# Attention with compressed values for two heads at once: a 256-column block diagonal, and its transposition in an earlier step and another bank

## The reference, cut to what matters

```python
kc = compress(k_cmp, pe_ck, w_ck1, w_ck2)      # 31 blocks, per group
vc = compress(v_cmp, pe_cv, w_cv1, w_cv2)
s_c = jnp.einsum('bqgrd,bngd->bgrqn', qb, kc)
p_c = masked_softmax(s_c, cmp_end[None, :] <= t[:, None])
o_cmp = jnp.einsum('bgrqn,bngd->bqgrd', p_c.astype(vc.dtype), vc)
...
out = gb[..., 0:1] * o_cmp + gb[..., 1:2] * o_sel + gb[..., 2:3] * o_win
```

## Time and profile before

| | us |
|---|---|
| median of 3 runs | 737.48 (737.27 to 737.51) |
| the profiled execution's own time | 737.37 |
| its span | 735.7 |
| PE busy in it | 721.4 (98%) |
| DVE, ACT, POOL busy | 511.6 (70%), 327.1 (44%), 149.7 (20%) |
| mean granted TensorE clock | 0.997 |

### The profile page before, as it was taken

The page is one execution under the profiler, slowest core; times in us unless marked ns, Lnnn a source line. Parts: engine busy times, 40 slices in busy tenths (PEclk is TensorE's granted clock), DMA queues, the critical chain, the costliest instruction groups (busy, mean ns, idle before and its releaser), DMA issues.

```text
span 735.7 us, 11843 instructions
## 1 busy us (share of the span) xinstructions
PE 721.4 (98%) x4379; PEld 640.1 (87%) x4379; DVE 511.6 (70%) x905; ACT 327.1 (44%) x528; POOL 149.7 (20%) x162
## 2 busy tenths in 40 slices
PE   8999999999999999999999999999999999999995
PEld 7889887888888997888879899999999998888884
DVE  3524187797778784675798779998898886233576
ACT  3513376567767676522324244444444353313500
POOL 2607080512333431000000212222222210000000
PEclk9999999999999999999999999999999999999998
DMA  8524325203011204633611123332233324232202
GB/s 258 166 89 136 94 66 157 65 1 98 19 57 58 58 1 112 231 112 132 214 58 58 58 67 105 114 114 86 86 114 114 114 88 160 95 114 80 92 29 86
DMA packets 57316, 72.79 MB, mean 99 GB/s; under 512 B 3872, under 2 KB 44352, under 8 KB 57280
## 3 DMA queue, kind: packets, MB, share of 16 engines
q1 hardware_dynamic: 57280, 72.32, 30.6%
HBM read 70.21 MB, written 2.10 MB: 98 GB/s over the span
## 4 chain that ended last, share of the span: by engine, by line
PE 89%; DVE 7%; ACT 2%; DMA 1%; issue 1%; SPq 0%; DVEq 0%; ACTq 0%
PE ps L1583 80%; PE ps L1595 4%; PE ps L1591 3%; PE ps L1592 3%; DMA arena<-in_x 1%; DVE y L1326 1%; DVE wl L1026 1%; DVE prob L1243 1%; ACT wh L660 1%; DVE y L1346 0%; DVE atl L1036 0%; DVE ptl L1036 0%; DVE stat L1305 0%; DVE y L1310 0%; DVE mix L1395 0%
## 5 line engine op out<-in xcount | busy, mean ns | idle before, releaser
L1583 PE MATMUL ps<-wh,xh 128*128 128x512 f32 (+1 forms) x376 | 145.0, 386 | 0.1
L1583 PE MATMUL ps<-wh,xl 128*128 128x512 f32 (+1 forms) x376 | 143.4, 381 | 0.0
L1583 PE MATMUL ps<-wl,xh 128*128 128x512 f32 (+1 forms) x376 | 143.2, 381 | 0.0
L1583 PE MATMUL ps<-xh,wh 128*128 128x256 f32 (+1 forms) x416 | 135.8, 327 | 1.1 <-DVE wl L1026 1.1
L1583 PE MATMUL ps<-xh,wl 128*128 128x256 f32 (+1 forms) x416 | 131.9, 317 | 0.0
L1583 PE MATMUL ps<-xl,wh 128*128 128x256 f32 (+1 forms) x416 | 131.6, 316 | 0.0
L1026 DVE TENSOR_TENSOR wl<-stage,wh 128x2048 fp32r<-128x2048 f32 (+1 forms) x29 | 66.0, 2276 | 93.3 <-ACT wh L666 64.0
L1583 PE MATMUL ps<-ath,wh 128*128 128x256 f32 (+1 forms) x280 | 86.1, 308 | 0.5 <-ACT hid_sg L919 0.5
L1583 PE MATMUL ps<-ath,wl 128*128 128x256 f32 (+1 forms) x280 | 86.0, 307 | 0.0
L1583 PE MATMUL ps<-atl,wh 128*128 128x256 f32 (+1 forms) x280 | 86.0, 307 | 0.0
L1583 PEld LDWEIGHTS ps<-xh,wl 128*128 128x128 f32 x416 | 79.3, 191 | 5.4
(11 more groups left out here) (285 smaller groups left out, 1354.1 us busy)
## 6 DMA issues: line engine op xcount, KB each, us to landing
stage<-in_w_in SPq DMA_DIRECT2D x28, 512.0 KB, 4.5
stage<-in_w_ffn_gate SPq DMA_DIRECT2D x22, 512.0 KB, 4.7
stage<-in_w_ffn_up SPq DMA_DIRECT2D x22, 512.0 KB, 4.4
stage<-in_w_ffn_down SPq DMA_DIRECT2D x22, 512.0 KB, 3.7
stage<-in_w_out SPq DMA_DIRECT2D x8, 512.0 KB, 4.7
arena<-in_x SPq DMA_DIRECT2D x8, 256.0 KB, 5.9
stage<-in_w_in SPq DMA_DIRECT2D x8, 256.0 KB, 6.1
stage<-in_w_branch_nsa SPq DMA_DIRECT2D x4, 512.0 KB, 7.0
```

The lines of the kernel that those rows point to most:

```text
L1583: return pe.matmul(out, (sh, sh, sl)[i], (mh, ml, mh)[i], start=start and i == 0, stop=stop and i == 2)
```

## The change

The values become one stationary operand for two heads. Rows of the compressed probabilities are now held in the head order 0, 2, 1, 3 (`HEAD_AT`), so that operand `vz[:, g, pr]` has the rows of both heads of pair `pr`, one in the upper, one in the lower half. The moving operands `pch` and `pcl` are now 128x256 with a block diagonal: the upper 64 rows of the transposition go to columns 0 to 127, the lower 64 to columns 128 to 255, the rest stays zero from one memset. A compressed step is two matmuls of 256 columns in place of four of 128. The high and the low part are each two instructions of 64x128 in place of one of 128x128.

The transposition of step `a` moves from iteration `a + 2` to iteration `a` (for the first, `a = 2`, it stays in iteration 4), and from bank 2 to bank 0. It therefore waits for the last scores in bank 0 to be read by DVE, and the next scores wait for `ct_lo`, that is for `pcl` to be written. On DVE and ACT the two instructions stand behind the probabilities' part of the same iteration.

```diff
+        HEAD_AT = (0, 2, 1, 3)
+        vz = vz_pc[:, 0:512].rearrange("p (g r c d) -> p g r c d", g=G, r=2, c=2)
+        pch, pcl = [vz_pc[:, 512 + 2 * P * i:512 + 2 * P * (i + 1)] for i in range(2)]
+        def pair_parts(t, bank):
+            return [(t[DH * a:DH * a + DH, P * a:P * a + P], bank[DH * a:DH * a + DH, 0:P]) for a in range(2)]
...
-        PT_BANKS = [1 - pr if br == 2 else (qt + 2) // 2 for qt, g, pr, br in STEPS]
+        PT_BANKS = [0 if br == 2 else (qt + 2) // 2 for qt, g, pr, br in STEPS]
+        CMP_AT = {(4 if a == 2 else a): a for a in range(N_STEPS) if STEPS[a][2:] == (0, 2)}
...  (ACT, iteration i, behind pth)
+                if i in CMP_AT:
+                    w = CMP_AT[i] // 6
+                    if w:
+                        act.wait_ge(pv_done, 6 * w)
+                    act.wait_ge(ct_done, w + 1)
+                    last = [hi(dst, src) for dst, src in pair_parts(pch, ps[:, 0, :])][-1]
+                    last.then_inc(ct_hi, 1)
...  (DVE, behind lo_prob(i - 2))
+            def lo_cmp(w):
+                dve.wait_ge(ct_hi, w + 1)
+                for (dst, src), (h, _) in zip(pair_parts(pcl, ps[:, 0, :]), pair_parts(pch, ps[:, 0, :])):
+                    last = lo(dst, src, h)
+                last.then_inc(ct_lo, 1)
...  (PE, ahead of the scores of step i)
+                    if i - 1 in CMP_AT:
+                        pe.wait_ge(ct_lo, CMP_AT[i - 1] // 6 + 1)
...  (PE, the product of step a = i - 3)
-                        pe.wait_ge(pt_lo, PT_BEFORE[a] + PT_BANKS[a])
-                        for hh in range(2):
-                            last = mm2(out[:, P * hh:P * hh + P], vz[:, g, 2 * pr + hh, :, :], pch[:, :], pcl[:, :],
-                                       False, hh == 1)
+                        pe.wait_ge(ct_lo, a // 6 + 1)
+                        last = mm2(out, vz[:, g, pr, :, :], pch, pcl, False, True)
...  (PE, behind the transposes of step i - 2)
-                    elif pr == 0:
-                        if a == 2:
-                            pe.wait_ge(pcmp_ok, 1)
-                        transpose(ps[:, PT0, 0:P],
-                                  pcmp[:, g, qt, :, :].rearrange("p k n -> p (k n)")).then_inc(pt_done, 1)
+                if i in CMP_AT:
+                    a = CMP_AT[i]
+                    qt, g, pr, br = STEPS[a]
+                    if a == 2:
+                        pe.wait_ge(pcmp_ok, 1)
+                    pe.wait_ge(s_max, 2 * SOFT[max(b for b in SOFT_STEPS if b <= i)] + 1)
+                    transpose(ps[:, 0, 0:P],
+                              pcmp[:, g, qt, :, :].rearrange("p k n -> p (k n)")).then_inc(ct_done, 1)
```

More of the change, by code:

```diff
@@ L140, in build_layer @@
         sgu_norm.close()
-        vz = sb("vz", [P, G, PAIRS, 2, DH], f32r, first)
+        vz_pc = sb("vz_pc", [P, 1024], f32r, first)
         sgu_mix = ExitStack()
@@ L160, in build_layer @@
         positional.close()
-        pch = sb("pch", [P, P], f32r, first)
-        pcl = sb("pcl", [P, P], f32r, first)
+        sb("behind_pe_in", [P, 2, P], fp32, first)
         pe_t = sb("pe_t", [P, 2, 16], fp32, first)
@@ L347, in build_layer @@
         pt_done, pt_hi, pt_lo = sem("pt_done"), sem("pt_hi"), sem("pt_lo")
+        ct_done, ct_hi, ct_lo = sem("ct_done"), sem("ct_hi"), sem("ct_lo")
         pv_done, o_hi, o_lo = sem("pv_done"), sem("o_hi"), sem("o_lo")
@@ L600, in _ @@
             pool.wait_ge(vln_ok, MT)
-            pool.memset(vz[:, :, :, :, :].rearrange("p a b c d -> p (a b c d)").bitcast(fp32), 0.0).then_inc(vz_zero, 1)
+            pool.memset(vz_pc[:, :].bitcast(fp32), 0.0).then_inc(vz_zero, 1)
             pool.wait_ge(w_lo, U_MERGE1 + 1)
@@ L800, in _ @@
                     r = slice(NB * j, NB * j + NB)
-                    hi(vz[r, g, j, g, :], ps[r, 3, DH * g:DH * g + DH]).then_inc(cmp_hi, 1)
+                    hi(vz[r, g, j % 2, g, :], ps[r, 3, DH * g:DH * g + DH]).then_inc(cmp_hi, 1)
             take_merge(2, U_MERGE1, False)
@@ L830, in _ @@
                         w = min(512, n - 512 * b)
[L831 to L834, removed]
+                        hi(pth[:, 512 * b:512 * b + w], ps[:, PT0 + b, 0:w]).then_inc(pt_hi, 1)
+                if i in CMP_AT:
[5 more added lines that the diff above has]
+                    last.then_inc(ct_hi, 1)
                 if i >= 5 and i % 3 == 2:
@@ L1150, in _ @@
                     dve.wait_ge(cmp_hi, G + G * (j + 1))
-                    lo(vz[r, g, j, 1 - g, :], ps[r, 3, DH * g:DH * g + DH], vz[r, g, j, g, :]).then_inc(cmp_lo, 1)
+                    lo(vz[r, g, j % 2, 1 - g, :], ps[r, 3, DH * g:DH * g + DH], vz[r, g, j % 2, g, :]).then_inc(cmp_lo, 1)
             dve.wait_ge(masks_ready, 4)
@@ L1186, in weigh_cmp @@
                     for g in range(G):
-                        step(dve.tensor_tensor(csum[:, g], csum[:, g], gates[:, :, g, :, 0], ALU.mult))
+                        by_head = csum[:, g].rearrange("p m (a b) -> p m b a", a=2)
+                        step(dve.tensor_tensor(by_head, by_head, gates[:, :, g, :, 0].rearrange(
+                            "p m (b a) -> p m b a", a=2), ALU.mult))
                 else:
@@ L1209, in lo_prob @@
                     part = slice(512 * b, min(512 * b + 512, n))
[L1210 to L1213, removed]
+                    lo(ptl[:, part], ps[:, PT0 + b, 0:part.stop - part.start], pth[:, part]).then_inc(pt_lo, 1)
+            def lo_cmp(w):
[3 more added lines that the diff above has]
+                last.then_inc(ct_lo, 1)
             def first_fill(part):
@@ L1252, in _ @@
                     lo_prob(i - 2)
+                if i in CMP_AT:
+                    lo_cmp(CMP_AT[i] // 6)
                 if i >= 5 and i % 3 == 2:
@@ L1745, in _ @@
                 for pp in range(PAIRS):
-                    pe.matmul(ps[:, g, :], kz[0][:, g, pp, :], q_t(g)[:, pp, :], start=pp == 0, stop=False)
-                    last = pe.matmul(ps[:, g, :], kz[1][:, g, pp, :], q_t(g)[:, pp, :], start=False,
+                    pe.matmul(ps[:, g, :], kz[0][:, g, pp, :], q_t(g)[:, HEAD_AT[pp], :], start=pp == 0, stop=False)
+                    last = pe.matmul(ps[:, g, :], kz[1][:, g, pp, :], q_t(g)[:, HEAD_AT[pp], :], start=False,
                                      stop=pp == PAIRS - 1)
```

## The result

The changed kernel takes 740.92 us (median of 5 runs, 740.53 to 741.88) against 737.33 us before (5 runs, 737.27 to 737.51): 1.0045 times as long, with a 95% interval of 1.0035 to 1.0056. Run again beside the experiments it took 740.94 against 737.49, a ratio of 1.0053 (1.0036 to 1.0069). It is 3.5 us slower.

The account below looks back on a forecast made before the run. PE, busy 98% of the span, was taken to bound the kernel. The terms -2.5 - 1.4 + 0.45 + 5.8 + 0.5 = +2.85 us on the median 737.48 gave 740.3 us, with a range of 737.8 to 742.9.

Parts of the forecast that it names:

- Part 1: Compressed product on PE: two matmuls of 256 columns save 0.155 us at each of 16 steps, 2.5 us less.
- Part 2: Compressed product's waits for `pcl`: all go with the transposition two or three iterations ahead, 1.4 us less.
- Part 3: Compressed transposition on PE, some 0.1 us at eight places, goes to another iteration: nothing in sum.
- Part 4: Iteration 4: the transposition waits for DVE to read scores from bank 0, 0.45 us more; later exponentials cost nothing.
- Part 5: Seven new waits of PE for `ct_lo` ahead of the scores, iterations 8 to 44: 5.8 us more.
- The restart: Slow restart of PE behind each of eight waits, 0.06 us each, 0.5 us more in all.
- Rival 1: Wait ahead of the scores is met in time, since the fill covers the chain: 734.1 us, chance 0.1.
- rival 2: DVE and ACT, freed of `pcl` and `pch`, run further ahead and absorb half the new wait: 736.9 us, chance 0.2.
- Rival 3: 256 columns cost what two matmuls of 128 do, so the wide product brings nothing: 742.8 us, chance 0.1.
- One sign of the prediction: In the changed profile, PE's busy time should be some 2 us lower while the span is longer.
- Late next: Transposes behind the compressed product wait for GpSimd's half of the probabilities: up to 0.3 us of the 1.4 lost.
- The sum: All terms over the whole kernel: +2.85 us, which gives 740.3 us.

Follow-up runs that it names:

- x1: Changed kernel with the transposition back in iteration `a + 2` and bank 2, so the wide product alone: 737.48 us, ratio 1.0004 against the kernel before.
- x3: Changed kernel with the compressed transposition in free bank 3 in the two small tiles, without the waits between it and the scores: 739.12 us, ratio 1.0019.
- x4: Changed kernel with compressed transposition, `pch` and `pcl` ahead of the same iteration's probabilities on PE, ACT and DVE: 736.56 us, ratio 0.9985 against the kernel before.
- x2: Kernel before with only the transposition moved early to bank 0, `pch` and `pcl` one instruction each, four matmuls of 128 columns: 740.61 us, ratio 1.0044.

## Why the prediction was right

The measured time lies in the range, 0.6 us above the forecast, and the mechanism is the one that was forecast: a cheaper product against a new wait ahead of the scores. That the sum comes so near is in part luck, as the last point shows.

- Part 1, 0.155 us for each product, measured 0.16. x1 shows it apart from the move. The 0.02 us a step that the upper bound had for the transposes behind came too, 0.35 us in all. By the isolated gap of the Trainium skill ("TensorE: Matmul & The Clock Gate", "Back-to-back issue gap"), 0.056 us at 128 columns, this part would have brought nearly nothing. The prediction used that formula without what the same section says of it: that it under-counts in a stream of loads and matmuls, for which it gives 0.081 us. Measured here are 0.11 us from one matmul of 128 columns to the next.
- Part 2, 1.4 us of waits: gone, but for 0.13 us at the first product, which still starts 0.05 us behind the end of `pcl`. The two terms together were forecast as 3.9 and measured as 3.85.
- Part 3, the moved transposition: nothing in sum, as forecast. It takes 0.11 us at the new place, and the fill matmuls behind the old one win as much.
- Part 4, iteration 4: 0.58 for 0.45. That its late exponentials cost nothing was wrong, and is the step that failed outright: "with more than a microsecond in hand" looked at the transposes. But DVE's normalisation waited for these exponentials, a merge weight of 1.22 us stands behind it and `ptl` of step 3 behind both, so `ptl` started 1.0 us later than before, the 0.3 us of offset left out, and its product waited 0.29 us. In x3, where the transposition of iteration 4 waits for nothing, this wait is gone.
- Part 5, the main one: each of the seven waits came at its place, within 0.1 us of the forecast, 5.5 for 5.8 in sum. x4 shows that they come from the compressed part standing behind the probabilities of the same iteration: with that order changed on PE, ACT and DVE the waits go. The prediction named `ptl` in DVE's queue. That is the last link at six of the seven places, though by the estimate under x4 it holds `pcl` for 2.3 us in all; in iteration 8 it holds nothing, and ACT's late `pch` sets the time, as the prediction had it there. x2 shows the second part of `pch` and `pcl` as 0.3 to 0.5 us of each.
- The restart was mis-sized: 0.11 us each in place of 0.06.
- Rival 1 (the wait is met) and rival 2 (half is absorbed) are refuted by the seven waits. Rival 3 is refuted by x1.
- One sign of the prediction did not come: PE's busy time was to be some 2 us lower, and is 0.3 lower. Of the 5.5 us of waits only 4.3 are listed as idle, and a restart or a transpose that comes late counts as busy.
- Late next, as feared: PE's transposes for POOL, 0.35 us. The product of step 45 waits 0.25 us for `ptl` since its own step comes 0.8 us earlier.
- The sum was 2.85 and came as 3.4. Too low or left out were 1.3 us: 0.29 + 0.25 for `ptl`, 0.35 for POOL, 0.24 of restarts, 0.13 in iteration 4. Against that stand 0.7 us: 0.3 less of waits, 0.35 for the second transposes, 0.1 that has no place. So errors of both signs cancelled in part.

## What to carry to other kernels

Before moving an operation to a buffer that the next step needs, ask when that buffer's last reader can be done: its place in each engine's queue, the instructions ahead of it, and what PE can do until then. A wait that is taken from a late use and put ahead of an earlier one is paid wherever the writer is not done by then, even if nothing is waiting there today; here the order within one iteration was worth more (4.4 us) than the cheaper matmuls (some 3 us). A form that saves the bound engine 0.16 us and gives the two that feed it 0.56 us more latency is only a gain where that latency is hidden.

## What the runs showed that I had not expected

- A semaphore that comes just in time still costs PE about 0.11 us: in x4 the shift stands at four of the seven scores with no idle time of PE, while 1.6 us of weight loads' waits for `pcl` are listed. The loads show where it goes. Before, the load of the first scores starts with the last fill matmul, and each further load with the matmul ahead of it. In x4 the load that waited starts together with its own matmul, and the next load 0.11 us behind it; the distance from that load to its matmul is 0.23 us in both, so the second matmul comes 0.34 us behind the first in place of 0.24. In iteration 15 of x4 the load starts 0.12 us ahead of its matmul, and the second matmul is not late. Before, and then x4:

```profile
214.82 0.19 PEld L1591 LDWEIGHTS ps<-ath 128*128 128x128 f32 x1
215.05 0.19 PEld L1592 LDWEIGHTS ps<-atl,ath 128*128 128x128 f32 x1
...
215.28 0.39 PE L1592 MATMUL ps<-atl,ath 128*128 128x512 f32 x1
```

```profile
215.16 0.19 PEld L1613 LDWEIGHTS ps<-ath 128*128 128x128 f32 x1 [0.29 <-DVE vz_pc L1050]
215.27 0.19 PEld L1614 LDWEIGHTS ps<-atl,ath 128*128 128x128 f32 x1
...
215.50 0.40 PE L1614 MATMUL ps<-atl,ath 128*128 128x512 f32 x1
```

- Two parts of 64 rows by 128 columns take ACT 0.53 us and DVE 0.58 us, where one of 128 by 128 took 0.27 and 0.29: half the rows cost the whole time each. The two parts do not overlap either: DVE's second starts 0.01 us behind the listed end of the first, where the second `ptl` starts 0.08 us ahead of it. The Trainium skill ("VectorE: DVE Perf Modes", "Two Vector instructions with no wait between them") has this hold for DVE, and the trace agrees. ACT's pair shows the same: 0.01 us behind, where its second `pth` starts 0.10 us ahead of the end of the first.
